# Expert layers of a fused two-block model: four front query blocks for eight, gathers in one run, gates behind the first dots, last unit in pairs

## The reference

```python
h = rmsnorm(x, norm_g)                             # 256 tokens x 1024
q = (h @ q_w).reshape(T, 8, 2, 128)                # 8 heads, two halves
s = einsum('thcd,ckd->thck', q, sub_keys)          # 128 scores per half
s1, i1 = top_k(s[:, :, 0], 16); s2, i2 = top_k(s[:, :, 1], 16)
cand_s = s1[..., :, None] + s2[..., None, :]       # 256 sums
best_s, best_pos = top_k(cand_s, 16)               # 16 experts of 16384
gate = softmax(best_s)
a = einsum('nd,nhkd->nhk', h, u[idx])
out = einsum('nhkd,nhk->nd', v[idx], gate * gelu(a))
```

## Time and profile before

| what | value |
|---|---|
| time, median of 3 runs | 3004.94 us (2997.56 to 3006.52) |
| profiled execution, its own time | 3008.61 us |
| its span | 3006.7 us, 34866 instructions |
| granted TensorE clock, mean | 0.926 |
| PE / DVE / ACT / POOL busy | 2548.0 / 1694.0 / 1183.8 / 942.7 us |
| gathers (q0, software_dynamic) | 73728 packets, 536.90 MB, 43.2% |
| weight ring and others (q1) | 65360 packets, 237.44 MB, 23.4% |

### The profile page before, as it was taken

How to read it: one execution, slowest core, us unless ns; L and a number is a source line. 1 busy time by engine, 2 the same in 40 slices (tenths; PEclk the granted TensorE clock), 3 DMA queues, 4 the chain that set the end, 5 groups by cost and what they waited for, 6 DMA issues and landing times.

```text
span 3006.7 us, 34866 instructions
## 1 busy us (share of the span) xinstructions
PE 2548.0 (85%) x11874; PEld 1815.3 (60%) x11874; DVE 1694.0 (56%) x3511; ACT 1183.8 (39%) x2562; POOL 942.7 (31%) x743
## 2 busy tenths in 40 slices
PE   7999899999789999878787878777877887786877
PEld 7988699899669977867543323333755443332334
DVE  4551355555455543555566767665465666677663
ACT  4446544434363446434333232333453332323233
POOL 0015400000230025535544333332525443333443
PEclk9999999999789989879899898999888999899898
DMA  5543255455325543314999999998417999999993
GB/s 191 183 167 120 92 187 184 167 185 184 103 78 183 183 139 126 126 64 142 378 418 414 421 420 421 418 416 341 153 59 294 408 411 419 421 418 417 417 413 143
DMA packets 141956, 783.48 MB, mean 261 GB/s; under 512 B 15872, under 2 KB 16384, under 8 KB 76288
## 3 DMA queue, kind: packets, MB, share of 16 engines
q0 software_dynamic: 73728, 536.90, 43.2%
q1 hardware_dynamic: 65360, 237.44, 23.4%
q10 hardware_dynamic: 2736, 7.46, 0.9%
HBM read 780.69 MB, written 1.05 MB: 260 GB/s over the span
## 4 chain that ended last, share of the span: by engine, by line
PE 47%; DMA 22%; DVE 12%; issue 7%; ACT 6%; POOL 6%; POOLq 0%; SPq 0%; DVEq 0%; ACTq 0%
DMA arena<-experts,arena 21%; PE ps L458 12%; PE ps L459 12%; PE ps L460 12%; PE ps L966 4%; PE ps L969 4%; POOL ring_lo L315 4%; DVE arena L2045 4%; ACT row L1421 2%; ACT arena L1414 1%; POOL arena L2150 1%; PE ps L880 1%; DVE ring_lo L315 1%; DVE arena L1540 0%; DVE hT_lo L1606 0%
## 5 line engine op out<-in xcount | busy, mean ns | idle before, releaser
L966 PE MATMUL ps<-arena,row 128*128 128x512 f32 x1024 | 574.4, 644 | 227.9 <-ACT row L1421 227.7
L2045 DVE SCALAR_TENSOR_TENSOR arena<-arena,ps 128x1024 f32<-128x1024 f32 x512 | 611.9, 1218 | 265.1 <-DMA arena<-experts,arena 264.9
L2150 POOL DMA_INDIRECT arena<-experts,arena x512 | 485.3, 948 | 735.0 <-PE ps L969 537.1
L458 PE MATMUL ps<-hT_hi,ring_hi 128*128 128x256 f32 x2048 | 603.7, 295 | 64.0 <-POOL ring_lo L315 56.8
L459 PE MATMUL ps<-hT_lo,ring_hi 128*128 128x256 f32 x2048 | 595.2, 291 | 0.0
L460 PE MATMUL ps<-hT_hi,ring_lo 128*128 128x256 f32 x2048 | 594.4, 290 | 0.0
L969 PE MATMUL ps<-arena,row 128*128 128x512 f32 x1024 | 557.6, 627 | 0.0
L315 POOL TENSOR_TENSOR ring_lo<-ring,ring_hi 128x1024 fp32r<-128x1024 f32 x180 | 429.6, 2394 | 347.6 <-ACT ring_hi L309 285.1
L309 ACT ACTIVATE ring_hi<-ring 128x1024 fp32r<-128x1024 f32 x448 | 462.9, 1057 | 141.5 <-PE ps L460 124.8
L966 PEld LDWEIGHTS ps<-arena,row 128*128 128x128 f32 x1024 | 197.5, 202 | 521.3 <-ACT row L1421 308.6
L458 PEld LDWEIGHTS ps<-hT_hi,ring_hi 128*128 128x128 f32 x2048 | 410.0, 200 | 74.4 <-issue 64.6
(11 more groups left out here) (270 smaller groups left out, 3003.7 us busy)
## 6 DMA issues: line engine op xcount, KB each, us to landing
ring<-stream SPq DMA_DIRECT2D x448, 512.0 KB, 3.8
arena<-experts,arena POOLq DMA_INDIRECT x512, 13.2
row<-rows_in ACTq DMA_DIRECT2D x11, 512.0 KB, 4.3
x<-x_in SPq DMA_DIRECT2D x1, 1024.0 KB, 5.0
out<-arena SPq DMA_DIRECT2D x2, 512.0 KB, 2.7
arena<-cols_in ACTq DMA_DIRECT2D x3, 256.0 KB, 2.7
cols<-cols_in SPq DMA_DIRECT2D x1, 425.5 KB, 5.6
arena<-cols_in ACTq DMA_DIRECT2D x1, 320.0 KB, 2.9
```

The costliest lines, as they stand in the source:

```text
L458: pe.matmul(dst, a[0], b[0], start=start, stop=False)
L966: lower = pe.matmul(ps[:, 2 * tb, :], diag, v[:, 0:HALF], start=first, stop=end)
L2045: last = dve.scalar_tensor_tensor(u, u, 1.0, h, ALU.mult, ALU.mult, accum_out=R["a"][:, n % 2, k:k + 1])
L2150: pool.indirect_dma_start(R["held"][:, g % HELD, :], None, experts, bass.IndirectOffsetOnAxis(ap=idx[:, n % 2, k:k + 1], axis=0))\
```

## The change

Four things are changed in both expert layers.

- `FRONT` is 4. The query blocks 4 to 15 are computed beside the groups of units 0 to 5. The copy of the second 128 input rows to PSUM moves from unit 4 to unit 6, since it uses banks that the queries use before.
- GpSimd makes the splits of the blocks 1 to 5, waits for the indices, and issues the 16 gathers of unit 0 with no split between. In later units it makes the split of block m + 2, not m + 1.
- `gates(n)` stands behind the dots of group 0 of the same unit, not at the end of the unit before.
- The last unit's groups are pairs, and the last two picks single: nine groups, not six.

```diff
-FINE = EVEN[:3] + [(12, 14), (14, 15), (15, 16)]
-FRONT = 8
+FINE = [(k, k + 2) for k in range(0, TOPK - 2, 2)] + [(14, 15), (15, 16)]
+FRONT = 4
@@ VectorE, peer
                 rows_in_psum(0)
-                gates(0)
                 for n in range(UNITS):
                     dots(n, 0)
+                    gates(n)
                     if n + 1 < UNITS:
                         top_keys(n + 1)
...
-                    if n == 4:
+                    if n == PH - 2:
                         dve.wait_ge(of("peer_qT"), SUBS * (l + 1))
                         rows_in_psum(1)
                     for group in range(3, len(groups_of(n))):
                         dots(n, group)
-                    if n + 1 < UNITS:
-                        gates(n + 1)
@@ GpSimd, expert_rows
-                for m in range(1, FRONT - 3):
+                for m in range(1, FRONT + 2):
                     make_lo(pool, base + m)
                 pool.wait_ge(of("peer_idx"), UNITS * l + 1)
-                gather(0, range(0, 4))
-                make_lo(pool, base + FRONT - 3)
-                gather(0, range(4, 8))
-                make_lo(pool, base + FRONT - 2)
-                gather(0, range(8, HELD))
-                make_lo(pool, base + FRONT - 1)
-                make_lo(pool, base + FRONT)
-                gather(0, range(HELD, TOPK))
+                gather(0, range(TOPK))
...
                         m = query_beside(n - 1, group)
-                        if m is not None and m + 1 < SUBS:
-                            make_lo(pool, base + m + 1)
+                        if m is not None and m + 2 < SUBS:
+                            make_lo(pool, base + m + 2)
                         gather(n, range(first, end))
```

## The result

| | before | after |
|---|---|---|
| median (lowest to highest), 5 runs each | 2999.56 (2996.76 to 3006.52) | 2978.99 us (2971.95 to 2982.23) |
| profiled execution: own time, span | 3008.61, 3006.7 | 2978.99, 2977.2 us |
| granted TensorE clock, mean | 0.926 | 0.925 |

The changed kernel takes 0.992 of the time before (95% interval 0.9899 to 0.9942), so it is 17 to 30 us faster. By the medians it is 20.6 us, by the means of the five runs each (3001.07 and 2977.16) 23.9. Of the 10.4 us between forecast and result, 5.4 are the starting point (the forecast set out from the median of three runs, 3004.94; with two more it is 2999.56) and 5.0 are the gain, forecast at 15.5. 20.6 is what the rival "no step pays" gives (20.5).

A forecast was written before the change was run, and what follows sets the result against it. It took full DMA in the two gather stages as the bound, with time lost at stage starts and in tails. 9.4 + 2.5 + 7.3 - 3.7 = 15.5 us off the median 3004.9 gave 2989.4, range 2980 to 3004.

The forecast's parts named there:

- no step pays: Rival: no unit change loses DMA time, since everything stands earlier; gain 20.5 us, time 2984.4, chance 0.13.
- the term of -3.7 us for the steps: Changes from one unit's gathers to the next's: late first gathers lose 5.0 us of DMA against 1.3 before.
- The bound: Both expert layers' gather stages: DMA is full, so only lost DMA time and the tail after the last landing can be gained.
- Start gap, 9.4: Start of both gather stages: four front blocks bring the first dots earlier, closing DMA gaps of 5.0 and 4.4 us.
- Ring loads, 2.5: Block 5's earlier split takes a 512 KB ring load out of the full DMA stretch: 1.25 us per layer.
- The dip that I took as proof: DMA loss of 1.3 us in peer1 at 2372, unit 1 to 2, read as what a late first gather costs.
- Tail, 7.3: Last unit in pairs: TensorE ends 5.0 us after the last dot starts, not 7.8 and 9.5; gain 2.8 + 4.5.
- Nothing for the gates' delay in 30 units: Gates behind first dots: table load later by 1.8 us per unit, first frees up to 4.2 us late, covered; no loss.
- The 7.7 us of queue: Gathers' median landing of 13.2 us against 5.5 at best, taken as cover for the gates' delay of 4.2 us.
- Nothing for breaks and for splits further ahead: GpSimd's first gathers without breaks and units' splits one block earlier: under full DMA, nothing gained.
- The starting point: Median of the runs before, 3004.9 us, from which the forecast subtracted its gain; the profiled execution took 3008.6.

The follow-up runs named there:

- e7: Kernel after with one extra, unread split on GpSimd ahead of each split before a unit's first gather, five per layer; ratio 0.9972 to the kernel before.
- e8: Kernel after with a unit's first two gathers issued ahead of the split, not the split ahead of all four; ratio 0.9901 to the kernel before.
- e5: Kernel before with only the gates moved behind the dots of group 0; ratio 0.9954 to the kernel before.
- e11: Kernel after with splits one block nearer and block 4's split between the first four gathers and the rest; ratio 0.9954 to the kernel before.
- e2: Kernel after with the gates back at the end of the unit before; 2974.40 us, ratio 0.992 to the kernel before.
- e9: Kernel after with ten slots for landed picks, not eleven; 2976.76 us, ratio 0.9931 to the kernel before.
- e10: Kernel after with nine slots for landed picks, not eleven; 3023.58 us, ratio 1.0104 to the kernel before.

## Why the prediction was wrong: the steps between units

The step of the prediction that failed is the term of -3.7 us for the steps. The runs showed a gain of 1.2 us in its place, since no step of the kernel after loses DMA time (the trace, e7 and e8); the other terms of the sum held. The other half of the 10.4 us is the starting point.

- **The bound** was read rightly: what shortened the stages was DMA time lost at their start, bytes, and the tail. 44.6 us less of GpSimd's waiting and 56.1 us less of TensorE's on L458 brought nothing by themselves.
- **Start gap, 9.4**: 9.5 measured, and the working held link by link (fourth dot, table load, diagonals and first free slot each within 0.7 us of the sum). What failed is whose gain it is. I gave it to the four front blocks alone and put the gates' move at nothing. Alone, that move shortens the front part by 5.3 us per layer, more than the gap of one (e5). With both in the change the total is the same, so the right number here is in part luck; a forecast for the gates' move alone would have come out wrong.
- **Ring loads, 2.5**: 2.6 by the bytes; e11 puts them back and pays.
- **The steps, -3.7: this is the term that failed.** I charged the kernel after 5.0 us at its steps and the kernel before 1.3. In the trace the losses outside the start went from 3.6 to 2.4 us, a gain of 1.2. The delay of the gather is as I gave it (from the dot of pick 11 to the gather 6.84 us, 6.7 forecast), and with four picks of cover it is about a microsecond too long. But the split that delays the gather also frees a ring slot, and the load that goes out at 2302.24 fills the 1.25 us. I had written that before, a queue of ring loads covered the step, and did not ask what load the step itself releases; before, too, each of these steps has a split and one load behind it. There are also five such splits per stage, not six: block 16 does not exist, which takes 0.6 of the 5.0. And the dip that I took as proof does not show a delay. Before, at 2372, the gather of pick 15 and the one of the next pick are these (GpSimd, then the time to landing of each):

```profile
2363.82 0.94 POOL L2150 DMA_INDIRECT arena<-experts,arena  x1 [5.62 <-PE ps L969]
2373.05 0.95 POOL L2150 DMA_INDIRECT arena<-experts,arena  x1 [0.16 <-issue]
...
DMA to landing us min/median/max: 12.4/12.4/12.4
...
DMA to landing us min/median/max: 6.9/6.9/6.9
```

They land at 2376.2 and 2379.9, 3.7 us apart, which is a gather and a ring load at full rate (2.49 + 1.25), just as at the step of the kernel after, which has no dip (2305.8 and 2309.5). The DMA share fell for 1.3 us there, and the landings were no later for it. Why, the rows do not show. e7 says that the fear was not idle: 2.2 of every further 2.4 us are paid.
- **Tail, 7.3**: 7.4 (4.97 and 4.96 us against 5.0 forecast).
- **Nothing for the gates' delay in 30 units**: right (e2). The 7.7 us of queue that I took as cover are not a measure of it; what e9 and e10 measure is that behind the delay 2.5 to 5 us of cover are left.
- **Nothing for breaks and for splits further ahead**: e11 undoes both together with the ring loads and leaves at most 1.8 us per stage for them.
- **The starting point, 5.4 us**: three runs of before had a median of 3004.94; of the three later groups none lies as high (3000.14, 3002.14, 2994.72). Against its own execution the forecast was 2993.1, and the profiled one of after took 2979.0: there the miss is 14.1, of which 5.2 are the gain (20.7 instead of 15.5), 3.3 stand outside the stages, 4.2 are the rate and 1.3 the remainder.

*What stays open.* By all traces a stage went from 679.5 us (mean of four stages in two profiles) to 666.4 (two stages), 13.1 us. Gap 4.3, middle 0.9, bytes 1.3 and tail 4.1, means of the same stages, account for 10.6 of it. The other 2.5 are of the size by which the rate of full DMA differs between executions of one kernel (418.1 to 420.4 GB/s in the kernel before, 0.5% or 3.6 us of a stage). Whether the change has a part in it, I did not settle.

## What to carry to other kernels

When an edit moves a wait, ask what it releases as well as what it delays: here the split that made the gathers late released the very transfer that, by the trace, filled the hole. A dip in a busy share is not yet a delay: look at when the transfers behind it land. When two edits of a change take away the same wait, each measured alone seems to bring most of the whole; only the four corners of the table show it. And a queue's slack is not the median landing less the fastest: take slots away and see.

## What the runs showed of the hardware that I had not expected

- Gathers land in the order of their issue, all 512 of them before and after. A ring load on the other queue does not keep to it: issued 0.02 us behind a gather, it landed 2.2 us before it (5.1 against 7.3 us to landing). It shifts the gathers behind it by its 1.2 us (3.70 against 2.49 us between dots).
- With nine gathers in flight the rate in the middle of a stage is 403 GB/s at a DMA share of 0.99 (387 and 395 in single windows of 20 us); with ten and eleven it is 417 at 1.01.
- TensorE's first two values matmuls take 2.07 us after 20.67 us of idle time, at a granted clock of 0.50 (1.2 GHz) over that window, and 1.02 at the end of the stage. GpSimd's gathers follow at 2.48 us once and then at 1.72, so about two picks are slow; the DMA share stays at 1.00 and more.
- The same program on the same chip differs by 0.6% between runs (2989.61 to 3008.12 in 23 runs of the kernel before), and the medians of three groups on three chips by 0.25%.
